# Moving thirteen of sixteen scalings by 1/rms from VectorE to GpSimd in two norm passages

## The chip, the cores and the metric

The kernel runs on one core of one Trainium2 chip. The metric is the device time of one execution in microseconds (us). The kernel before took 3422.58 us, the median of three runs between 3416.58 and 3427.88 us. PE is TensorE, PEld its weight loads, DVE is VectorE, ACT is ScalarE, POOL is GpSimd, SP is SyncE, which here issues the DMAs.

## The reference

A block of three layers on one sequence of 512 tokens with 2048 channels: an S5 layer, a FoX attention layer, and a layer that mixes dilated attention with RWKV-7. Two of the places between them matter here. Each of the first two layers ends with a projection whose output is normed and added to the residual stream, and what comes next norms the sum again:

```
def rmsnorm(x, g):
    xf = x.astype(F32)
    y = xf * lax.rsqrt(jnp.mean(xf * xf, axis=-1, keepdims=True) + RMS_EPS)
    return (y * g.astype(F32)).astype(x.dtype)
...
return h + rmsnorm(y @ w_out, g_post)     # end of the S5 layer
kvf = rmsnorm(h, g_kv) @ w_kv             # what reads it next
...
return h + rmsnorm(o @ w_out, g_post)     # end of the FoX layer
h = rms_norm(x, norm_g[l])                # what reads it next
proj = jnp.matmul(h, w_in[l])
```

## The kernel before

All activations lie transposed: 2048 channels are 16 blocks of 128 partitions, and each block is 128x512 (512 tokens), f32. `g1` holds the residual stream h in 16 blocks, `g2` the projection's output in 16 blocks. A projection works on 228 weight tiles of 128x2048, one after the other. To get the accuracy of f32 from TensorE's fp32r matmuls, the weight tile and the activations are each split in a high part (rounded, by ACT: `whi`, `rhi`) and a low part (the rest: `wlo`, by GpSimd in `make_lo`; `rlo`, by DVE), and each 128x128 piece of a tile takes three matmuls (`project`, L158 to L160). A tile's two buffers alternate.

The two norm passages lie around tile 64 (`N_GATE`, the forget gate's weights, passage 1) and tile 145 (`N_LORA`, passage 2). Each goes like this:

- PE sums the squares over the partitions (L660), ACT takes the root (L664), DVE the reciprocal (L669). In the passages the reciprocal is written to a PSUM bank, `banks[6]`, and not back to `rstd` in SBUF.
- DVE runs `residual_and_split`: for block k it adds the scaled output to the residual (L769), scales the next block (`scaled(k+1)`, L763, `g2` times `banks[6]`), and, once ACT has rounded the new residual to `rhi` (L791 or L793), subtracts to get `rlo` (L774 in passage 1, L776 with the gain in passage 2).
- ACT runs `split_after_update`: when a block of the residual is up, it makes `rhi` and the block's square (L795).
- PE runs `project_summing`: for each block, once `rlo` is there, three matmuls of the tile, and one with ones that sums the squares of the next norm (L784). PE does nothing else in the passage.

Semaphores order the engines; each engine runs its own list, written out by hand. `h_sc` counts scaled blocks, `h_up` added ones, `r_hi` and `r_lo` the split parts. On GpSimd's list, passage 1 has `make_lo` of tile 65 and then `scale_w` of tile 66, which multiplies the weights with a gain (L839, four instructions). Passage 2 has `make_lo` of tile 146; `make_lo` of tile 147 waits for ACT, which makes that tile's `whi` after the passage.

What follows the passages: after passage 1, ACT's root, DVE's reciprocal and the gate's chain come ahead of ACT's `whi` of tile 66 (L139), GpSimd's `wlo` of it, and then PE's tile. After passage 2, SP waits for `r_lo`, stores h to HBM (L1874) and loads tables, for which DVE's first step of the third layer waits.

Of the kernel before, what the change touches and what calls it, by code (L numbers as in the profile page):

```python
# [17 lines left out]
ALU = mybir.AluOpType  # L18
# [6 lines left out]
KT = D // P  # L25
# [48 lines left out]
def program(nc, a):  # L74
    ctx = ExitStack()
    with ctx:
# [3 lines left out]
        def sem(name):  # L80
            return ctx.enter_context(nc.semaphore(name))
# [8 lines left out]
        g2 = sb("g2", [P, KT * T])  # L90
# [3 lines left out]
        rstd = sb("rstd", [P, T])  # L94
# [4 lines left out]
        banks = [bank[:, i, :] for i in range(8)]  # L99
# [41 lines left out]
        def make_lo(pool, n, slot):  # L141
            pool.wait_ge(w_hi, n + 1)
            for q in range(QUARTERS):
                c = slice(q * D // QUARTERS, (q + 1) * D // QUARTERS)
                ins = pool.tensor_tensor(wlo[:, slot, c], wraw[:, slot, c], whi[:, slot, c].bitcast(F32), ALU.subtract)  # L145
            ins.then_inc(w_lo, 1)
# [97 lines left out]
        def col(base, k):  # L244

            if isinstance(k, int):
                return base[:, k * T:(k + 1) * T]
            return base[:, bass.ts(k, T)]
# [418 lines left out]
        def norm_recip(d, link, which, out=None):  # L667
            d.wait_ge(st_sd, which + 1)
            d.reciprocal(rstd[:, :] if out is None else out, rstd[:, :]).then_inc(st_rd, 1)  # L669
            d.wait_ge(st_rd, which + 1)  # L670
# [5 lines left out]
        h_sc = sem("h_sc")  # L676
# [76 lines left out]
        def dve_out_squares(d, n0, sbase):  # L753
            dve_square(d, 0, n0 % 2, sbase, first=True)
            dve_square(d, 1, (n0 + 1) % 2, sbase)
            with d.Fori(0, 7) as i:
                for u in range(2):
                    dve_square(d, 2 * i + (2 + u), (n0 + u) % 2, sbase)

        def residual_and_split(d, n, hbase, rgain, rbase):  # L760

            def scaled(k):
                d.tensor_tensor(col(g2, k), col(g2, k), banks[6], ALU.mult).then_inc(h_sc, 1)  # L763
            d.wait_ge(evac, n + 2)
            scaled(0)
            for k in range(KT):
                c = col(g1, k)
                d.wait_ge(h_sc, hbase + k + 1)
                d.tensor_tensor(c, c, col(g2, k), ALU.add).then_inc(h_up, 1)  # L769
                if k < KT - 1:  # L770
                    scaled(k + 1)
                d.wait_ge(r_hi, rbase + k + 1)
                if rgain is None:
                    d.tensor_tensor(rlo[:, k, :], c, rhi[:, k, :].bitcast(F32), ALU.subtract).then_inc(r_lo, 1)  # L774
                else:
                    d.scalar_tensor_tensor(rlo[:, k, :], c, vec[:, rgain + k:rgain + k + 1],  # L776
                                           rhi[:, k, :].bitcast(F32), ALU.mult, ALU.subtract).then_inc(r_lo, 1)
# [54 lines left out]
        def scale_w(pool, n, slot, half, gain):  # L832

            pool.wait_ge(w_in[slot], 16 * half + 16)
            raw = wraw[:, slot, :].rearrange("p (k c) -> p k c", k=KT)
            for q in range(QUARTERS):
                k = slice(q * KT // QUARTERS, (q + 1) * KT // QUARTERS)
                g = vec[:, gain + q * KT // QUARTERS:gain + (q + 1) * KT // QUARTERS]
                ins = pool.tensor_tensor(raw[:, k, :], raw[:, k, :], bc(g, 2, [P, KT // QUARTERS, P]), ALU.mult)  # L839
            ins.then_inc(w_sc, 1)  # L840
# [1051 lines left out]
        @block.gpsimd  # L1892
        def _(pool):
            pool.memset(ones[:, :], 1.0).then_inc(t_zero, 1)
            pool.wait_ge(cst, 48)
            for n in range(EARLY + 1):
                make_lo(pool, n, n % 2)
            pool.wait_ge(pw_rdy, 1)
            for v in range(2):
                pool.memset(m8b[v].rearrange("q (g k) -> q g k", g=GT)[:, :, 0:1], 0.0)  # L1900
            pool.memset(m["tt"], 0.0).then_inc(t_zero, 1)
            pool.wait_ge(t_zero, 2)
            steps(pool, pool_step)
            tile_pairs(pool, 32, 62, pool_lo)
            for n in (62, 63):
                make_lo(pool, n + 1, 1 - n % 2)
                scale_w(pool, n + 2, n % 2, (n + 2) // 2, V_GKV)
            make_lo(pool, 65, 1)
            scale_w(pool, 66, 0, 33, V_GKV)
            with pool.Fori(0, KT - 1) as h:  # L1910
                fox_pool(pool, h)
            fox_pool(pool, KT - 1, last=True)
            tile_pairs(pool, 130, 146, lambda p, n, u, h, j: make_lo(p, n, u))
            make_lo(pool, 146, 0)
            make_lo(pool, 147, 1)
            tile_pairs(pool, 148, 152, lambda p, n, u, h, j: make_lo(p, n, u))
            make_lo(pool, 152, 0)
            with pool.Fori(0, 7) as p:
                rw_pool(pool, p, True)
            rw_pool(pool, 7, False)  # L1920
            make_lo(pool, 213, 1)
            at_pool(pool)
            tile_pairs(pool, 214, 228, lambda p, n, u, h, j: make_lo(p, n, u))
# [85 lines left out]
        @block.vector  # L2009
        def _(d):  # L2010
            link = Chain(d, vch)
            d.sem_inc(evac, 2)
            d.sem_inc(a_wr, 16)
            d.wait_ge(cst, 48)
            parameters(d, link, 0)
            split_lo(d, g1, V_G1, 0, (sqb0, 0))
            norm_recip(d, link, 0)
            parameters(d, link, 1)
            d.wait_ge(e_wr, 16)
            d.wait_ge(t_zero, 2)  # L2020
            steps(d, dve_step, link, DVE_U_LINKS)
            d.wait_ge(z_rdy, 15)
            d.wait_ge(gemm, N_GLU)
            d.tensor_tensor(zt, acc[1][:, :], rstd[:, :], ALU.mult).then_inc(evac, 1)
            split_lo(d, g1, None, 16)
            d.wait_ge(z_in, 32)
            d.wait_ge(z_rdy, KT)
            tile_pairs(d, 32, 48, lambda d, n, u, h, j: dve_glu(d, link, n, u, h, j), link, 2)
            split_lo(d, g2, None, 32)
            dve_out_squares(d, N_WO, 16)  # L2030
            norm_recip(d, link, 1, banks[6])
            d.wait_ge(x_in, 64)
            residual_and_split(d, N_GATE, 0, None, 48)
            norm_recip(d, link, 2)
            gate_dve(d, link)
            d.wait_ge(msk_in, 16)
            fox_dve(d, link, 0, False)
            fox_dve(d, link, 1, True)
            with d.Fori(2, KT) as h:
                link.enter(h - 2, 4)  # L2040
                fox_dve(d, link, h, True)
                link.leave(KT - 2)
            softmax_max(d, link, KT - 1)
            split_lo(d, g2, None, 64, ks=range(0, 6))
            softmax_divide(d, link, KT - 1)
            split_lo(d, g2, None, 64, ks=range(6, 10))
            gate_out(d, KT - 1)
            split_lo(d, g2, None, 64, ks=range(10, KT))
            dve_out_squares(d, N_FO, 48)
            norm_recip(d, link, 3, banks[6])  # L2050
            residual_and_split(d, N_LORA, 16, V_G2, 80)
            norm_recip(d, link, 4)

            link(d.memset(w["u"][:, 0:1], 0.0))
            d.wait_ge(x_out, 64)
            d.wait_ge(p6_in, 96)
            for i, name in enumerate(("wa", "sg0", "sg1")):
                shift_mix(d, link, N_LORA + i, (N_LORA + i) % 2, vec[:, V_MU + i:V_MU + i + 1], w[name], lo_u, (lo_u, i))
            d.wait_ge(lo_u, 3)
            for i in range(3):  # L2060
                rw_inputs(d, link, 0, i)
            rw_z(d, 0)
            d.memset(xt["zt3"], 0.0)
            for name in ("rcos", "rsin"):
                ins = d.tensor_tensor(xt[name], xt[name], rstd[:, :], ALU.mult)
            link(ins)
            with d.Fori(0, 7) as p:
                link.enter(p, RW_LINKS)
                rw_dve(d, link, p, True)
                link.leave(7)  # L2070
            rw_dve(d, link, 7, False)
            at_dve(d, link)
            d.wait_ge(x_in, 80)
            dve_last(d, link, 212, 0, 0, 80, first=True)
            dve_last(d, link, 213, 1, 1, 80)
            d.wait_ge(f_x, 48)
            tile_pairs(d, 214, 228, lambda d, n, u, h, j: dve_last(d, link, n, u, j + 2, 80))
            norm_recip(d, link, 5)
            for k in range(KT):
                c = g1[:, k * T:(k + 1) * T]  # L2080
                d.scalar_tensor_tensor(c, c, vec[:, V_GF + k:V_GF + k + 1], rstd[:, :], ALU.mult, ALU.mult)\
                 .then_inc(f_r, 1)
# [191 lines left out]
```

## Time and profile before

| | |
|---|---|
| median of three runs | 3422.58 us |
| the profiled execution | 3420.76 us |
| its span in the trace | 3418.9 us |
| PE busy | 3244.8 us (95%) |
| DVE busy | 1400.2 us (41%) |
| ACT busy | 1119.1 us (33%) |
| POOL busy | 1657.1 us (48%) |

The busy share of an engine is over the whole span. The two passages are short stretches of it: from PE's sum of squares to its last L784 they lie at 936 to 979 us and at 1991 to 2035 us. A row of the timeline tells when an instruction started, how long it took from its start to its end, and in brackets how long its engine sat idle before it and what ended that. The duration of an instruction holds the time in which it had started and waited for its operands' port.

### The profile page before, as it was taken

How to read it: one execution, taken by the hardware profiler on the slowest of the kernel's cores; microseconds unless marked ns; L12 is line 12 of the kernel's file. 1: busy time of each engine (PE TensorE's matmuls, PEld its weight loads, DVE VectorE, ACT ScalarE, POOL GpSimd, SP SyncE). 2: the span in 40 equal slices, each digit the busy share in tenths (PEclk: the TensorE clock that was granted, in tenths of full speed). 3: DMA queues.
4: the chain of work that ended last, by engine and by line, in shares of the span. 5: the costliest groups of instructions: out<-in, count | busy, mean ns of one | idle time of the engine just before them, and what ended most of it. 6: DMA issues, size and time to landing. Idle time of an engine off the chain costs nothing.

```text
span 3418.9 us, 48576 instructions
## 1 busy us (share of the span) xinstructions
PE 3244.8 (95%) x18636; PEld 2523.1 (74%) x18636; DVE 1400.2 (41%) x2138; ACT 1119.1 (33%) x1472; POOL 1657.1 (48%) x1315
## 2 busy tenths in 40 slices
PE   5899998999989999999998978999999999999997
PEld 3688886878757877877887856777777777774686
DVE  8877784120052222222312043444445445355512
ACT  4344443233333233223323233233233233234421
POOL 2466652444547776776663414443344344442242
PEclk9899998999999999999999999999999999997999
DMA  3555556232212222222221222222222222223322
GB/s 132 153 147 163 165 159 171 98 136 98 98 50 87 82 78 86 86 84 76 86 86 63 97 108 99 82 77 83 81 96 75 83 84 83 75 84 107 115 94 91
DMA packets 122898, 341.60 MB, mean 100 GB/s; under 512 B 59408, under 2 KB 62480, under 8 KB 91664
## 3 DMA queue, kind: packets, MB, share of 16 engines
q1 hardware_dynamic: 122768, 339.67, 30.1%
q8 instruction: 106, 1.74, 0.2%
q14 instruction: 24, 0.20, 0.0%
HBM read 301.09 MB, written 33.82 MB: 98 GB/s over the span
## 4 chain that ended last, share of the span: by engine, by line
PE 80%; issue 10%; POOL 5%; DVE 4%; ACT 2%; DMA 0%; ACTq 0%; SPq 0%; POOLq 0%; DVEq 0%
PE bank L158 22%; PE bank L160 21%; PE bank L159 20%; POOL wlo L145 4%; PE bank L1321 3%; PE bank L1629 2%; PE bank L1008 1%; PE bank L1026 1%; PE bank L421 1%; PE bank L420 1%; ACT whi L139 1%; PE bank L1630 1%; PE bank L406 1%; PE bank L432 1%; PE bank L1704 1%
## 5 line engine op out<-in xcount | busy, mean ns | idle before, releaser
L145 POOL TENSOR_TENSOR wlo<-wraw,whi 128x512 fp32r<-128x512 f32 x912 | 1245.4, 1397 | 1473.6 <-ACT whi L139 1473.5
L158 PE MATMUL bank<-rhi,whi 128*128 128x512 f32 x3648 | 1494.3, 410 | 109.2 <-POOL wlo L145 38.6
L159 PE MATMUL bank<-rlo,whi 128*128 128x512 f32 x3648 | 1433.4, 393 | 0.0
L160 PE MATMUL bank<-rhi,wlo 128*128 128x512 f32 x3648 | 1432.7, 393 | 0.0
L158 PEld LDWEIGHTS bank<-rhi,whi 128*128 128x128 f32 x3648 | 691.7, 190 | 326.7 <-issue 91.1
L160 PEld LDWEIGHTS bank<-rhi,wlo 128*128 128x128 f32 x3648 | 691.7, 190 | 149.6
L159 PEld LDWEIGHTS bank<-rlo,whi 128*128 128x128 f32 x3648 | 693.1, 190 | 140.9 <-issue 11.3
L139 ACT ACTIVATE whi<-wraw 128x2048 fp32r<-128x2048 f32 x228 | 436.9, 1916 | 624.4 <-PE bank L160 479.9
L839 POOL TENSOR_TENSOR wraw<-wraw,vec 128x512 f32<-128x512 f32 x260 | 266.1, 1055 | 0.0
L751 DVE TENSOR_TENSOR ssum<-ssum,wk 128x512 f32<-128x512 f32 x30 | 21.6, 719 | 311.8 <-ACT wk L741 311.8
L741 ACT ACTIVATE wk<-bank 128x512 f32<-128x512 f32 x32 | 27.9, 871 | 238.0 <-PE bank L160 238.0
L1321 PEld LDWEIGHTS bank<-g 64*64 64x64 f32 x2560 | 82.0, 134 | 30.2 <-issue 29.4
L1530 POOL TENSOR_TENSOR g<-g,wk 128x256 f32<-128x256 f32 x80 | 58.4, 752 | 91.9 <-PE bank L1321 66.1
L1215 DVE TENSOR_TENSOR g<-g,bank 128x256 f32<-128x256 f32 x80 | 32.4, 405 | 161.9 <-PE bank L1321 161.6
L1321 PE MATMUL bank<-g 64*64 64x64 f32 x2560 | 93.6, 221 | 0.2
L913 DVE SCALAR_TENSOR_TENSOR wk<-bank,rstd 128x512 f32<-128x512 f32 x16 | 11.1, 692 | 200.1 <-PE bank L160 200.1
L918 DVE TENSOR_TENSOR wk<-bank,rstd 128x512 f32<-128x512 f32 x16 | 11.1, 692 | 168.7 <-PE bank L160 168.7
L728 DVE TENSOR_TENSOR wk<-wk,g 128x512 f32<-128x512 f32 x16 | 11.1, 693 | 149.2 <-ACT wk L724 142.0
L1480 ACT ACTIVATE g<-bank 128x256 f32<-128x256 f32 x80 | 30.7, 384 | 124.2 <-PE bank L1321 121.5
L929 ACT ACTIVATE wk<-wk 128x128 f32<-128x128 f32 (+1 forms) x64 | 35.2, 551 | 108.5 <-DVE wk L887 108.5
L1100 DVE TENSOR_TENSOR wk<-bank,rstd 128x512 f32<-128x512 f32 x27 | 18.6, 691 | 117.5 <-PE bank L160 104.3
L1809 DVE TENSOR_TENSOR g<-g,bank 128x512 f32 (+1 forms) x16 | 11.0, 688 | 135.4 <-PE bank L160 135.4
(361 smaller groups left out, 3277.9 us busy)
## 6 DMA issues: line engine op xcount, KB each, us to landing
wraw<-in_wall_dram SPq DMA_DIRECT2D x228, 1024.0 KB, 4.8
g<-in_bmat_dram SPq DMA_DIRECT2D x16, 512.0 KB, 5.5
g<-scr_e SPq DMA_DIRECT2D x128, 64.0 KB, 4.8
scr_a<-ssum SPq DMA_DIRECT2D x24, 256.0 KB, 2.1
g<-in_xp_dram SPq DMA_DIRECT2D x4, 1024.0 KB, 12.5
g<-in_cmat_dram SPq DMA_DIRECT2D x16, 256.0 KB, 4.5
scr_u<-wk SPq DMA_DIRECT2D x16, 256.0 KB, 5.8
scr_y<-wk SPq DMA_DIRECT2D x16, 256.0 KB, 2.2
```

The lines of the kernel that those rows point to most:

```text
L139: act.activation(whi[:, slot, :], wraw[:, slot, :], ACT.Copy).then_inc(w_hi, 1)
L145: ins = pool.tensor_tensor(wlo[:, slot, c], wraw[:, slot, c], whi[:, slot, c].bitcast(F32), ALU.subtract)
L158: pe.matmul(acc[slot][:, :], whk, rhi[:, k, :], start=(k == 0), stop=False)
L159: pe.matmul(acc[slot][:, :], whk, rlo[:, k, :], start=False, stop=False)
L160: ins = pe.matmul(acc[slot][:, :], wlk, rhi[:, k, :], start=False, stop=(k == KT - 1))
L406: ins = pe.matmul(ps_k[g // 4][0:SC, (g % 4) * P:(g % 4 + 1) * P], m["bb"][:, g * SC:(g + 1) * SC], q1[v][:, g * 144:g * 144 + P], start=T ...
L420: pe.matmul(ps_y[:, cols], m["tt"][:, g * P:(g + 1) * P], ug[u][:, cols], start=True, stop=False)
L839: ins = pool.tensor_tensor(raw[:, k, :], raw[:, k, :], bc(g, 2, [P, KT // QUARTERS, P]), ALU.mult)
L929: ins = act.activation(sc, sc, ACT.Exp, bias=mf["nm"][:, b:b + 1], accum_out=mf["sum"][:, b:b + 1])
L1321: ins = pe.matmul(to[hs_[e], b * CH:(b + 1) * CH], lhs[hs_[e], b * CH:(b + 1) * CH], rhs[hs_[e], b * CH:(b + 1) * CH], start=True, stop=True)
L1530: pool.tensor_tensor(ml[hd].rearrange("p (b t) -> p b t", b=NB), ab4[hd][:, :, 0], bc(lv, 1, [P, NB, CH]), ALU.mult).then_inc(rw_ml, 1)
L1629: pe.matmul(to, at_q[u][hs_[hd], b * P:(b + 1) * P], at_k[u][hs_[hd], 0:n], start=True, stop=False)
```

## The change

From the fourth block on (k of 3 to 15), GpSimd does the scaling in both passages. DVE keeps the scaling of blocks 0 to 2, all additions and all low parts. GpSimd's new piece stands in its list behind `make_lo` of tile 65 and ahead of `scale_w` of tile 66 in passage 1, and behind `make_lo` of tile 146 in passage 2. It starts when DVE's three scalings have counted `h_sc` up. The reciprocal goes back to `rstd` in SBUF, and all scalings, those on DVE too, read it there.

```
+        OWN = 3
+
+        def scaled(eng, k):
+            eng.tensor_tensor(col(g2, k), col(g2, k), rstd[:, :], ALU.mult).then_inc(h_sc, 1)
+
+        def scale_out(pool, hbase):
+            pool.wait_ge(h_sc, hbase + OWN)
+            for k in range(OWN, KT):
+                scaled(pool, k)
+
         def residual_and_split(d, n, hbase, rgain, rbase):
 
-            def scaled(k):
-                d.tensor_tensor(col(g2, k), col(g2, k), banks[6], ALU.mult).then_inc(h_sc, 1)
             d.wait_ge(evac, n + 2)
-            scaled(0)
+            scaled(d, 0)
             for k in range(KT):
                 c = col(g1, k)
                 d.wait_ge(h_sc, hbase + k + 1)
                 d.tensor_tensor(c, c, col(g2, k), ALU.add).then_inc(h_up, 1)
-                if k < KT - 1:
-                    scaled(k + 1)
+                if k + 1 < OWN:
+                    scaled(d, k + 1)
                 d.wait_ge(r_hi, rbase + k + 1)
...
             make_lo(pool, 65, 1)
+            scale_out(pool, 0)
             scale_w(pool, 66, 0, 33, V_GKV)
...
             make_lo(pool, 146, 0)
+            scale_out(pool, 16)
             make_lo(pool, 147, 1)
...
-            norm_recip(d, link, 1, banks[6])
+            norm_recip(d, link, 1)
...
-            norm_recip(d, link, 3, banks[6])
+            norm_recip(d, link, 3)
```

DVE's list before, from the reciprocal of passage 1 (L763 scales, L769 adds, L774 makes the low part):

```order
L669 RECIPROCAL bank<-rstd 128x512 [waits st_sd]
L763 TENSOR_TENSOR g<-g,bank 128x512 [waits evac,x_in,st_rd]
L769 TENSOR_TENSOR g<-g 128x512 [waits h_sc]
L763 TENSOR_TENSOR g<-g,bank 128x512
L774 TENSOR_TENSOR rlo<-g,rhi 128x512 [waits r_hi]
L769 TENSOR_TENSOR g<-g 128x512 [waits h_sc]
```

The same place in the changed kernel, where the addition is L777 and the low part L782:

```order
L669 RECIPROCAL rstd<-rstd 128x512 [waits st_sd]
L763 TENSOR_TENSOR g<-g,rstd 128x512 [waits evac,x_in,st_rd]
L777 TENSOR_TENSOR g<-g 128x512 [waits h_sc]
L763 TENSOR_TENSOR g<-g,rstd 128x512
L782 TENSOR_TENSOR rlo<-g,rhi 128x512 [waits r_hi]
L777 TENSOR_TENSOR g<-g 128x512 [waits h_sc]
L763 TENSOR_TENSOR g<-g,rstd 128x512
L782 TENSOR_TENSOR rlo<-g,rhi 128x512 [waits r_hi]
L777 TENSOR_TENSOR g<-g 128x512 [waits h_sc]
L782 TENSOR_TENSOR rlo<-g,rhi 128x512 [waits r_hi]
L777 TENSOR_TENSOR g<-g 128x512 [waits h_sc]
L782 TENSOR_TENSOR rlo<-g,rhi 128x512 [waits r_hi]
```

After the third scaling DVE's list is additions and low parts in turn, each with its wait.

GpSimd's list before, at passage 1 (L145 is `make_lo`, L839 is `scale_w`):

```order
L145 TENSOR_TENSOR wlo<-wraw,whi 128x512 [waits w_hi]
L145 TENSOR_TENSOR wlo<-wraw,whi 128x512 x3
L839 TENSOR_TENSOR wraw<-wraw,vec 128x512 [waits w_in0]
L839 TENSOR_TENSOR wraw<-wraw,vec 128x512 x3
L1910 UNCONDITIONAL_BRANCH
```

The same place in the changed kernel, where `scale_w` is L847:

```order
L145 TENSOR_TENSOR wlo<-wraw,whi 128x512 [waits w_hi]
L145 TENSOR_TENSOR wlo<-wraw,whi 128x512 x3
L763 TENSOR_TENSOR g<-g,rstd 128x512 [waits h_sc]
L763 TENSOR_TENSOR g<-g,rstd 128x512 x12
L847 TENSOR_TENSOR wraw<-wraw,vec 128x512 [waits w_in0]
L847 TENSOR_TENSOR wraw<-wraw,vec 128x512 x3
L1919 UNCONDITIONAL_BRANCH
```

Thirteen instructions come in between, each with both inputs in SBUF, and one wait, for DVE's third scaling.

## Rows read from the trace of the kernel before

**Rows 1.** Timeline of all engines, one block of passage 1, GpSimd idle: start us, duration us, engine
```profile
955.36 0.68 DVE L769 TENSOR_TENSOR g<-g 128x512 f32<-128x512 f32 x1
955.50 0.50 PE L158 MATMUL bank<-rhi,whi 128*128 128x512 f32 x1 [0.17 <-DVE rlo L774]
...
955.96 0.68 DVE L763 TENSOR_TENSOR g<-g,bank 128x512 f32<-128x512 f32 x1
956.08 0.63 ACT L791 ACTIVATE rhi<-g 128x512 fp32r<-128x512 f32 x1 [0.84 <-DVE g L769]
...
956.31 1.02 PE L784 MATMUL bank<-wk,ones 128*128 128x512 f32 x2
...
956.74 0.69 DVE L774 TENSOR_TENSOR rlo<-g,rhi 128x512 fp32r<-128x512 f32 x1
957.35 0.69 DVE L769 TENSOR_TENSOR g<-g 128x512 f32<-128x512 f32 x1
```

**Rows 2.** Timeline of DVE, blocks of passage 2, GpSimd idle
```profile
2013.61 0.69 DVE L769 TENSOR_TENSOR g<-g 128x512 f32<-128x512 f32 x1
...
2015.08 0.75 DVE L776 SCALAR_TENSOR_TENSOR rlo<-g,vec,rhi 128x512 fp32r<-128x512 f32 x1 [0.19 <-ACT rhi L793]
2015.75 0.68 DVE L769 TENSOR_TENSOR g<-g 128x512 f32<-128x512 f32 x1
```

**Rows 3.** Timeline of GpSimd, passage 1, and two of its instructions apart
```profile
939.88 5.84 POOL L145 TENSOR_TENSOR wlo<-wraw,whi 128x512 fp32r<-128x512 f32 x4 [3.09 <-ACT whi L139]
945.68 5.83 POOL L839 TENSOR_TENSOR wraw<-wraw,vec 128x512 f32<-128x512 f32 x4
...
942.33 3.39 POOL L145 TENSOR_TENSOR wlo<-wraw,whi 128x512 fp32r<-128x512 f32 x2
```

**Rows 4.** Timeline of DVE, passage 1, while GpSimd works
```profile
941.43 0.69 DVE L763 TENSOR_TENSOR g<-g,bank 128x512 f32<-128x512 f32 x1
...
947.64 1.52 DVE L769 TENSOR_TENSOR g<-g 128x512 f32<-128x512 f32 x1
949.09 0.67 DVE L763 TENSOR_TENSOR g<-g,bank 128x512 f32<-128x512 f32 x1
...
950.54 1.52 DVE L769 TENSOR_TENSOR g<-g 128x512 f32<-128x512 f32 x1
```

**Rows 5.** Instructions by line on GpSimd, duration ns: least, median, most
```profile
L485 POOL TENSOR_TENSOR wk<-wk,g x16: 1301/1524/2335, 107.1 to 508.2; 128x512 f32<-128x512 f32 x16
L839 POOL TENSOR_TENSOR wraw<-wraw,vec x260: 1033/1041/1488, 921.2 to 1768.2; 128x512 f32<-128x512 f32 x130
L145 POOL TENSOR_TENSOR wlo<-wraw,whi x912: 1255/1288/3682, 16.0 to 3383.3; 128x512 fp32r<-128x512 f32 x183
```

**Rows 6.** Timeline of DVE, passage 1: the low part of block 9
```profile
964.70 0.69 DVE L774 TENSOR_TENSOR rlo<-g,rhi 128x512 fp32r<-128x512 f32 x1
```

**Rows 7.** Timeline of GpSimd and DVE, start of passage 2
```profile
1995.04 5.84 POOL L145 TENSOR_TENSOR wlo<-wraw,whi 128x512 fp32r<-128x512 f32 x4 [7.91 <-ACT whi L139]
1996.59 0.69 DVE L763 TENSOR_TENSOR g<-g,bank 128x512 f32<-128x512 f32 x1
```

**Rows 8.** Timeline behind passage 1: what waits for its end
```profile
979.25 0.69 ACT L664 ACTIVATE rstd<-bank,vec 128x512 f32<-128x512 f32 x1 [2.11 <-PE bank L784]
...
994.82 0.79 PE L158 MATMUL bank<-rhi,whi 128*128 128x512 f32 x1 [4.70 <-POOL wlo L145]
```

**Rows 9.** Timeline behind passage 2
```profile
2034.95 3.42 SPq L1874 DMA_DIRECT2D scr_x<-g  x4
...
2062.08 0.80 PE L158 MATMUL bank<-rhi,whi 128*128 128x512 f32 x1 [16.31 <-POOL wlo L145]
```

**Rows 10.** Stretches of passage 1: us, PE, PEld, DVE, ACT, POOL busy, granted clock, DMA
```profile
950.00:953.00 3.00, 1.93 (x6) 0.86 (x5) 2.90 (x4) 1.26 (x3) 1.51 (x2) 1.00 0.01 3
```

**Rows 11.** Timeline of PE, first block of passage 1, at the low clock
```profile
944.74 0.77 PE L158 MATMUL bank<-rhi,whi 128*128 128x512 f32 x1 [7.66 <-DVE rlo L774]
946.16 1.91 PE L784 MATMUL bank<-wk,ones 128*128 128x512 f32 x2
```

## The prediction

> **What bounds the kernel now.** I read the page first: PE is busy for 95% of the span, so a change to DVE's and GpSimd's work counts only where PE waits for them. In the two norm passages it does. There the timeline is read block by block. In a block of passage 1 with GpSimd idle [rows 1] PE starts at 955.50 after 0.17 us of waiting for DVE's `rlo`, and its last matmul ends at 956.31 + 1.02 = 957.33, so a block costs PE 1.83 us. The blocks follow each other at 957.35 - 955.36 = 1.99 us. What sets 1.99 is a loop through ACT: DVE starts the addition at 955.36, ACT starts `rhi` at 956.08, DVE starts `rlo` at 956.74 (1.38 after the addition), and the next addition at 957.35. DVE's scaling lies at 955.96 to 956.64, inside the wait for ACT's `rhi`, which ends at 956.08 + 0.63 = 956.71. It ends 0.1 us before `rlo` can start and so costs nothing. In passage 2 the same holds with more room [rows 2]: the period is 2015.75 - 2013.61 = 2.14 us, and `rlo` still waits 0.19 us for ACT behind the scaling.
>
> A second thing is to be seen where GpSimd works beside DVE [rows 3, 4]. The addition, which needs 0.68 us alone, takes 1.52 us, and two of them follow at 950.54 - 947.64 = 2.90 us. GpSimd's four instructions of L839 take 5.83 us there, 1.45 each, where one takes 1.04 alone [rows 5]. In one block DVE does two instructions with both inputs in SBUF (addition and `rlo`) and GpSimd two of its own, and 2 x 1.45 = 2.90: they take turns, one waiting for the other. The scaling, which reads PSUM, stays at 0.67 us in the same stretch [rows 4]. The Trainium skill states this as a rule (SBUF — State Buffer, "Who interferes with whom"): a DVE instruction with two SBUF inputs and a GpSimd instruction that reads SBUF share one read port, which the first one holds for its whole instruction. By that rule, the trace agrees, and it speaks against this change, which gives DVE's scalings a second SBUF input and puts thirteen more port holders beside DVE.
>
> **What the change removes.** Thirteen DVE scalings per passage, at 0.60 us of DVE's time each. I cost their removal at 0, because the loop through ACT stays as it is and covers them [rows 1, 2]: without them DVE waits 0.78 us for ACT instead of 0.17. The reciprocal keeps its size and its place; I cost its new target at 0.
>
> **What it adds on GpSimd.** Thirteen multiplications 128x512 with two full inputs. Nearest rows: L839, whose second input is a repeated vector, 1.04 us alone; L145, two full inputs, 1.26 us; L485, two full inputs and an f32 output, 1.30 us [rows 5]. Taking turns with DVE, two instructions of L145 need 945.72 - 942.33 = 3.39 us less the overlap of 0.04 [rows 3], that is 1.67 each; L839 needs 1.45; L485 by 1.30 plus the same 0.42 of DVE's hold would need 1.72 or 1.75. I take 1.67, since two full inputs are what the new ones have, and keep 1.45 and 1.75 as the ends. [...]
>
> GpSimd takes two blocks in the time in which DVE takes one, so it is never late with a block. What it does is to lengthen DVE's loop from 1.99 or 2.14 to 3.34 us for as long as it works.
>
> **Passage 1.** The start: GpSimd's `make_lo` of tile 65 runs from 939.88 [rows 3], with boundaries at 942.33, 944.0 (halfway) and 945.7 once each instruction has DVE's turn in it. DVE's scaling of block 0, ready at 941.43 [rows 4], now gets the port at 942.33, the addition at 944.0, the scaling of block 1 at 945.7. Then at DVE's own spacing of 0.61: `rlo` of block 0 at 946.33, addition 1 at 946.94, the scaling of block 2 at 947.55, done at 948.23. GpSimd starts there, and `rlo` of block 1, ready 1.38 after its addition at 948.32, comes just behind it. From 948.25 on there are 13 instructions at 1.67 and the 4 of `scale_w` at 1.45, together 27.5 us; two go to a block, so `rlo` of block 9 gets its port after the seventeenth, at 948.25 + 27.5 - 0.42 = 975.3. Before, it started at 964.70 [rows 6], `scale_w`'s contention included. From block 10 on the pace is 1.99 again. Passage 1: **+10.6**.
>
> **Passage 2.** GpSimd's `make_lo` starts at 1995.04 and DVE's first scaling at 1996.59 [rows 7]; the same reckoning (port at 1997.48, 1999.2, 2000.88) ends the third scaling at 2003.45. Before, GpSimd was then idle. Thirteen at 1.67 less 0.42 end at 2024.7, where `rlo` of block 7 gets its port; before it started at 2015.08 [rows 2]. Passage 2: **+9.7**.
>
> **Does it reach the end?** PE waits for `rlo` in nearly every block, so its last L784 moves with the last `rlo`. Behind passage 1 ACT's root waits for that matmul, and the gate's chain leads from there to the `wlo` for which PE waits 4.70 us until 994.82 [rows 8]. Behind passage 2 the stores start at 2034.95, when the last low part and sums are there, and PE waits 16.31 us for what follows from them [rows 9]. No slack takes the delay up. GpSimd's delayed work costs nothing: `scale_w` of tile 66 ends near 976, and ACT wants it after the gate's chain; `make_lo` of tile 147 waits for ACT until after passage 2. No DMA issue moves: `wlo` of tile 65 still comes ahead of the new piece, and it alone frees the buffer.
>
> **The sum.** +10.6 + 9.7 = +20.3, on the profiled 3420.76 gives 3441.1. The median of the runs is 1.8 above the profiled execution, so it is 3442.9, rounded 3443. With 1.45 in place of 1.67 it is 26 x 0.22 = 5.7 less (+14.6), with 1.75 it is 2.1 more (+22.4). With the runs' own scatter of 5 to 6 us this case reaches from 3433 to 3450.
>
> **Rivals.** (a) *The clock falls too.* In the long contended stretch PE works 1.83 of 3.34 us. In the one like it before it worked 1.93 of 3.00 us at a granted clock of 1.00 [rows 10], and the changed one is thinner. At half clock a block takes PE 946.16 + 1.91 - 944.74 = 3.33 us [rows 11], which hides behind 3.34; but if the clock is still low for the first two free blocks, each costs 1.34 more (1.19 in passage 2). That is +5.1 over both passages, less what PE regains at 0.16 and 0.31 per later block, so about +4: 3447. For it: the clock is at 0.50 when the passages begin, and PE is idle more. Against it: the clock stayed high in that stretch. The Trainium skill (TensorE: Matmul & The Clock Gate, "What's actually happening") says that a low rate comes from too little recent activity; no run here yet shows this stretch.
>
> (b) *The port isn't what slows DVE*, and the 1.52 us are of those weight tiles alone. Then only the start costs, addition 1 at 946.94 in place of the time when it got its port, 945.7, thus 1.2 per passage: 3425, no change that can be measured. Against it: the addition takes 1.52 us beside GpSimd and 0.68 without it [rows 1, 4], the scaling from PSUM doesn't grow, and GpSimd's own grow from 1.04 to 1.45.
>
> (c) *Faster: DVE is the bound of the passage, not ACT's loop.* If `rlo` could follow earlier with the scaling gone, the pace would fall to PE's own 1.83: 13 x (1.99 - 1.83) + 13 x (2.14 - 1.83) = 6.1 less, 3416.5. It decides once GpSimd's instructions take turns without holding DVE up, and `rlo` no longer waits for `rhi`. Against it are the 0.19 us of waiting for ACT in each block of passage 2 [rows 2], even with the scaling there.
>
> That the change doesn't do what it says can be left out: the lists show it.
>
> **Chances.** The forecast 0.75, (a) 0.13, (b) 0.08, (c) 0.04. A measurement of this kernel tells 0.3% (10.3 us) from no change. Slower by more than that: nearly all of the forecast (its low end, +14.6, less scatter can fall under 10.3, some 0.03) and all of (a): 0.85. Within 0.3%: (b) and that edge, 0.11. Faster: 0.04, and that only counts (c) with scatter on its side. The range reaches past the forecast's own on both sides for (a) and scatter: 3431 to 3453; (b) and (c) are left out with 0.12.
>
> **What would show it.** Right: additions of 1.5 to 1.8 us for blocks 2 to about 8 or 9, GpSimd's L763 at about 1.7 each, 13 in a row right behind DVE's third scaling, a pace of 3.3 us, then 1.99 and 2.14 unchanged to the end; the last L784 of passage 1 some 10 us later. Wrong: L763 on GpSimd at 1.5 or less (a smaller sum), additions at 0.68 us beside it (b), a pace under 1.99 us anywhere (c), a granted clock of 0.50 within the passage (a). A delay that is there in the passages and not behind them would mean that I missed slack.

## The result and the profile after

The changed kernel takes 3442.71 us, the median of seven runs (3440.9 to 3449.59), against 3422.58 us for the kernel before on the same chip (seven runs, 3416.58 to 3429.13). The ratio is 1.0059, with a 95% interval of 1.0047 to 1.0071: slower by 20 us, or 0.6%. The profiled execution took 21.5 us longer by its span (3440.4 against 3418.9 us).

DVE's timeline of passage 1 after the change (L763 scales, L777 adds, L782 makes the low part):

```profile
941.99 1.49 DVE L763 TENSOR_TENSOR g<-g,rstd 128x512 f32<-128x512 f32 x1
943.51 1.63 DVE L777 TENSOR_TENSOR g<-g 128x512 f32<-128x512 f32 x1
945.07 1.75 DVE L763 TENSOR_TENSOR g<-g,rstd 128x512 f32<-128x512 f32 x1
946.74 0.68 DVE L782 TENSOR_TENSOR rlo<-g,rhi 128x512 fp32r<-128x512 f32 x1
947.35 0.68 DVE L777 TENSOR_TENSOR g<-g 128x512 f32<-128x512 f32 x1
947.95 0.68 DVE L763 TENSOR_TENSOR g<-g,rstd 128x512 f32<-128x512 f32 x1
948.72 1.80 DVE L782 TENSOR_TENSOR rlo<-g,rhi 128x512 fp32r<-128x512 f32 x1
...
953.81 1.77 DVE L777 TENSOR_TENSOR g<-g 128x512 f32<-128x512 f32 x1
956.28 0.98 DVE L782 TENSOR_TENSOR rlo<-g,rhi 128x512 fp32r<-128x512 f32 x1 [0.70 <-ACT rhi L799]
957.18 1.77 DVE L777 TENSOR_TENSOR g<-g 128x512 f32<-128x512 f32 x1
...
975.76 0.75 DVE L782 TENSOR_TENSOR rlo<-g,rhi 128x512 fp32r<-128x512 f32 x1 [0.70 <-ACT rhi L799]
976.43 0.68 DVE L777 TENSOR_TENSOR g<-g 128x512 f32<-128x512 f32 x1
977.81 0.69 DVE L782 TENSOR_TENSOR rlo<-g,rhi 128x512 fp32r<-128x512 f32 x1 [0.70 <-ACT rhi L799]
978.42 0.68 DVE L777 TENSOR_TENSOR g<-g 128x512 f32<-128x512 f32 x1
```

GpSimd's timeline of the same passage:

```profile
940.45 5.83 POOL L145 TENSOR_TENSOR wlo<-wraw,whi 128x512 fp32r<-128x512 f32 x4 [3.09 <-ACT whi L139]
948.71 21.47 POOL L763 TENSOR_TENSOR g<-g,rstd 128x512 f32<-128x512 f32 x13 [2.44 <-DVE g L763]
970.14 5.82 POOL L847 TENSOR_TENSOR wraw<-wraw,vec 128x512 f32<-128x512 f32 x4
```

While GpSimd scales, the additions take 1.77 us and follow at 957.18 - 953.81 = 3.37 us; once GpSimd is done with `scale_w`, at 975.96, they take 0.68 us and follow at 978.42 - 976.43 = 1.99 us, as before [rows 1]. In that last part DVE waits 0.70 us for ACT in every block: the time of the scalings that it no longer does has turned into waiting. No row of DVE waits for a block that GpSimd has scaled. GpSimd's thirteen take 21.47 us, 1.65 each on average. The first two scalings on DVE, which read PSUM and took 0.69 us before [rows 4], now take 1.49 and 1.75 us beside `make_lo`.

To measure a passage I take the time from the start of the reciprocal ahead of it to the start of the reciprocal behind it. Of passage 1 and of passage 2 after the change:

```profile
938.60 3.35 DVE L669 RECIPROCAL rstd<-rstd 128x512 f32<-128x512 f32 x1 [2.14 <-ACT rstd L664]
...
991.11 3.35 DVE L669 RECIPROCAL rstd<-rstd 128x512 f32<-128x512 f32 x1 [2.65 <-ACT rstd L664]
2004.00 3.35 DVE L669 RECIPROCAL rstd<-rstd 128x512 f32<-128x512 f32 x1 [1.94 <-ACT rstd L664]
...
2055.97 3.35 DVE L669 RECIPROCAL rstd<-rstd 128x512 f32<-128x512 f32 x1 [2.63 <-ACT rstd L664]
```

and of the kernel before:

```profile
938.04 3.36 DVE L669 RECIPROCAL bank<-rstd 128x512 f32<-128x512 f32 x1 [2.14 <-ACT rstd L664]
...
979.97 3.35 DVE L669 RECIPROCAL rstd<-rstd 128x512 f32<-128x512 f32 x1 [2.62 <-ACT rstd L664]
1993.20 3.36 DVE L669 RECIPROCAL bank<-rstd 128x512 f32<-128x512 f32 x1 [1.94 <-ACT rstd L664]
...
2035.62 3.35 DVE L669 RECIPROCAL rstd<-rstd 128x512 f32<-128x512 f32 x1 [2.63 <-ACT rstd L664]
```

From start to start, passage 1 grew from 41.93 to 52.51 us (+10.6) and passage 2 from 42.42 to 51.97 us (+9.6), together 20.1 us. All that lies outside, the span less these two, went from 3334.6 to 3335.9 us. What comes behind a passage kept its length. These are PE's first matmuls after the wait behind passage 1 and behind passage 2, in the changed kernel:

```profile
1005.96 0.79 PE L158 MATMUL bank<-rhi,whi 128*128 128x512 f32 x1 [4.69 <-POOL wlo L145]
2082.26 0.80 PE L158 MATMUL bank<-rhi,whi 128*128 128x512 f32 x1 [16.12 <-POOL wlo L145]
```

From the second reciprocal to them it is 14.85 and 26.29 us, against 14.85 and 26.46 before [rows 8, 9].

### The profile page after: what moved, and what is told of

Its sections match the earlier page's. It is cut to its first block, busy times and chain, and to the rows that moved or that the text cites. A ratio compares the mean times of both kernels' runs of the same rounds, so it can differ in the third digit from the quotient of the medians.

```text
span 3440.4 us, 48576 instructions
## 1 busy us (share of the span) xinstructions
PE 3245.5 (94%) x18636; PEld 2523.4 (73%) x18636; DVE 1403.4 (41%) x2112; ACT 1119.3 (33%) x1472; POOL 1700.0 (49%) x1341
## 4 chain that ended last, share of the span: by engine, by line
PE 80%; issue 9%; POOL 5%; DVE 5%; ACT 2%; DMA 0%; ACTq 0%; SPq 0%; POOLq 0%; DVEq 0%
PE bank L158 22%; PE bank L159 21%; PE bank L160 21%; POOL wlo L145 3%; PE bank L1329 3%; PE bank L1637 2%; POOL g L763 1%; PE bank L1016 1%; PE bank L1034 1%; PE bank L421 1%; PE bank L420 1%; PE bank L1638 1%; PE bank L406 1%; PE bank L432 1%; ACT whi L139 1%
## 5 line engine op out<-in xcount | busy, mean ns | idle before, releaser
L145 POOL TENSOR_TENSOR wlo<-wraw,whi 128x512 fp32r<-128x512 f32 x912 | 1245.2, 1396 | 1446.1 <-ACT whi L139 1446.1
L847 POOL TENSOR_TENSOR wraw<-wraw,vec 128x512 f32<-128x512 f32 x260 | 266.1, 1055 | 0.0
```

## The experiments

The table gives for each kernel the two stretches just described, what they differ by from before (84.35 us together), and the span outside of them; these are from one profiled execution of each kernel. The times are medians of 4 (e5) to 12 (e7) runs. Each ratio is to the runs of before on the same chip, whose median was 3421.85 us beside e1 to e4, 3422.00 beside e5 to e7 and 3418.69 beside e8.

| kernel | passage 1, us | passage 2, us | together | outside | time, us | ratio, 95% interval |
|---|---|---|---|---|---|---|
| before | 41.93 | 42.42 | | 3334.6 | 3422.58 | |
| changed | 52.51 | 51.97 | +20.1 | 3335.9 | 3442.71 | 1.0059 [1.0047, 1.0071] |
| e1_nobody_scales | 41.92 | 42.42 | 0.0 | 3336.3 | 3424.38 | 1.0001 [0.9989, 1.0013] |
| e2_extra_multiplications | 48.23 | 48.20 | +12.1 | 3336.4 | 3436.09 | 1.0038 [1.0023, 1.0053] |
| e3_writes_only | 42.58 | 42.43 | +0.7 | 3334.3 | 3422.63 | 1.0007 [0.9997, 1.0018] |
| e4_all_on_dve_from_sbuf | 44.52 | 43.67 | +3.8 | 3342.0 | 3431.14 | 1.0022 [1.0011, 1.0034] |
| e5_two_buffers | 51.29 | 50.70 | +17.6 | 3342.2 | 3443.47 | 1.0052 [1.0034, 1.0070] |
| e6_own_nine | 48.37 | 48.29 | +12.3 | 3335.1 | 3436.28 | 1.0043 [1.0027, 1.0060] |
| e7_addition_ahead | 38.12 | 39.22 | -7.0 | 3333.6 | 3412.54 | 0.9981 [0.9968, 0.9993] |
| e8_one_per_block | 50.42 | 48.98 | +15.1 | 3332.2 | 3435.59 | 1.0051 [1.0035, 1.0067] |

The medians move by several us for a reason outside of the passages (last section), so the readings rest on the two stretches, and the times only bear them out.

**e1: is the removal worth anything?** The kernel before, without the scalings of blocks 3 to 15, which are added unscaled:

```
-                d.wait_ge(h_sc, hbase + k + 1)
+                if k < 3:
+                    d.wait_ge(h_sc, hbase + k + 1)
...
-                if k < KT - 1:
+                if k + 1 < 3:
                     scaled(k + 1)
```

> The kernel before, but blocks 3 to 15 of the projection's output are added unscaled in both passages: DVE does only the scalings of blocks 0 to 2, from PSUM, and GpSimd gets nothing new. The scaling of 13 blocks is left out. Theory (DVE's scaling is hidden behind ACT's rounding of the same block): paces stay 1.99 us in passage 1 and 2.14 us in passage 2, the last low part starts where it did, the time is that of before within 2 us (3422). Rival (DVE is the bound of the passage, so that taking scalings off it gains): the pace falls towards 1.83 us, 6 us less, 3416.

Both stretches are the same to 0.01 us. DVE's timeline in passage 1:

```profile
958.20 0.68 DVE L770 TENSOR_TENSOR g<-g 128x512 f32<-128x512 f32 x1
959.58 0.69 DVE L775 TENSOR_TENSOR rlo<-g,rhi 128x512 fp32r<-128x512 f32 x1 [0.70 <-ACT rhi L792]
960.19 0.68 DVE L770 TENSOR_TENSOR g<-g 128x512 f32<-128x512 f32 x1
```

With nothing between the addition and the low part the period is still 960.19 - 958.20 = 1.99 us, and where the scaling lay DVE now idles 0.70 us until ACT's `rhi` is there. So the removal alone, with nothing new on GpSimd, is worth nothing.

**e2: does GpSimd's work cost if nobody needs it?** The kernel before, with 13 multiplications more on GpSimd in each passage, on a scratch tensor:

```
+        NX = 13
...
+        def extra(pool, hbase, base):
+            pool.wait_ge(h_sc, hbase + 3)
+            for i in range(NX):
+                pool.wait_ge(ex, base + i)
+                pool.tensor_tensor(scr[:, :], scr[:, :], scr[:, :], ALU.mult).then_inc(ex, 1)
```

> The kernel before, with all scalings on DVE from PSUM, plus 13 GpSimd multiplications 128x512 per passage on a scratch tensor of their own, in the place of the new scalings, started by DVE's third scaling. DVE never waits for their data. Theory (they take turns with DVE at a shared SBUF port): the contended blocks follow at 3.3 us, additions take 1.5 to 1.8 us, +9 us in passage 1 and +8 us in passage 2 against before, since DVE's own scalings read PSUM and the start stays as it was; 3439 to 3440. Rival (DVE is late in the changed kernel because it waits for blocks that GpSimd has scaled, by semaphore): here there is no such wait, 3422 to 3425.

The stretches grew by 6.3 and 5.8 us, without DVE waiting for any result of GpSimd: the mechanism is as expected, its size is not. The reason is in the instruction itself (GpSimd, durations in ns, least, median and most):

```profile
L786 POOL TENSOR_TENSOR scr<-scr x26: 1039/1368/1465, 946.4 to 2026.8; 128x512 f32<-128x512 f32 x26
```

A multiplication whose two inputs are the same buffer takes 1.04 us at the least, like L839 with its repeated vector, and not the 1.26 us of L145 [rows 5]. That left open whether those of the changed kernel take longer because they read two buffers.

**e5: the same with two buffers.** One change against e2 (and a wait on ACT behind the passage, for the buffer's sake):

```
-                pool.tensor_tensor(scr[:, :], scr[:, :], scr[:, :], ALU.mult).then_inc(ex, 1)
+                pool.tensor_tensor(scr[:, :], scr[:, :], whi[:, slot, 0:512].bitcast(F32), ALU.mult).then_inc(ex, 1)
```

> e2 again, with one thing changed: the 13 extra GpSimd multiplications read two different buffers (scratch and a piece of whi), where those of e2 read the same buffer twice. In e2 each took 1.41 us beside DVE, in the changed kernel 1.65. Theory (GpSimd's price hangs on how many operands it fetches through the port): 1.65 us each, +8.8 us in passage 1 and +7.8 us in passage 2 over before, 3438 to 3440. Rival (the 1.65 us of the changed kernel come from something in its g2 blocks or semaphores): 1.41 us again, +12 us in all, 3434.

GpSimd's timeline, passage 1:

```profile
947.72 21.47 POOL L786 TENSOR_TENSOR scr<-scr,whi 128x512 f32<-128x512 f32 x13 [1.22 <-DVE g L766]
```

The thirteen take 21.47 us, to the hundredth what the changed kernel's own take. The stretches grew by 9.4 and 8.3 us, 17.6 together, where 16.6 were expected. The time of 3443.47 us lies above the 3438 to 3440 expected; the last section looks at that. So 17.6 of the 20.1 us are there when DVE's arithmetic is just as before and all it has to bear is a neighbour that reads two buffers.

**e3: is it reading, or any work of GpSimd's?** As e2, but with 34 memsets, which read nothing:

```
+        NX = 34
...
+            for i in range(NX):
+                pool.wait_ge(ex, base + i)
+                pool.memset(scr[:, :], 1.0).then_inc(ex, 1)
```

> The kernel before plus 34 GpSimd memsets 128x512 per passage, which write SBUF and read nothing, in the same place and for about as long (16 to 20 us of GpSimd). Theory (what is contended for is the read port of DVE's second SBUF input): the memsets leave DVE alone, additions stay at 0.68 us behind make_lo, and the time is that of before within 2 us, 3422 to 3425. Rival (any GpSimd instruction on SBUF holds DVE up, or GpSimd's semaphores do): additions of 1 us and more, +8 to +17 us, 3431 to 3440.

GpSimd is busy for 19.78 us of passage 1, and DVE does not notice:

```profile
946.49 19.78 POOL L786 MEMSET scr<- 128x512 f32 x34 [1.21 <-DVE g L766]
```

```profile
957.10 0.68 DVE L772 TENSOR_TENSOR g<-g 128x512 f32<-128x512 f32 x1
957.70 0.68 DVE L766 TENSOR_TENSOR g<-g,bank 128x512 f32<-128x512 f32 x1
958.48 0.69 DVE L777 TENSOR_TENSOR rlo<-g,rhi 128x512 fp32r<-128x512 f32 x1
959.09 0.68 DVE L772 TENSOR_TENSOR g<-g 128x512 f32<-128x512 f32 x1
```

The period is 1.99 us, passage 2 grew by 0.01 us and passage 1 by 0.65. The growth of passage 1 is no work of the memsets: `scale_w` comes later there, behind them, at 966.24, and its first instruction holds up a low part that would have taken 0.69 us:

```profile
966.45 1.38 DVE L777 TENSOR_TENSOR rlo<-g,rhi 128x512 fp32r<-128x512 f32 x1
```

The memsets wrote SBUF all that time, and GpSimd waited for a semaphore before each. So what costs is GpSimd's reading.

**e4: what does reading rstd in SBUF cost?** The changed kernel with `OWN = KT` and without the two calls of `scale_out`:

```
-        OWN = 3
+        OWN = KT
```

> The changed kernel with all 16 scalings on DVE, nothing new on GpSimd: what is left of the change is that the scalings read rstd in SBUF and not the PSUM bank. Theory: only the stretches in which GpSimd does make_lo and scale_w beside DVE cost more, because DVE's scalings now take turns too: about +3 us in passage 1 (it still has scale_w) and +1.5 us in passage 2, 3426 to 3428. The paces with GpSimd idle stay 1.99 and 2.14 us. Rival (most of the 20 us comes from reading rstd in SBUF): 3435 or more.

The stretches grew by 2.6 and 1.3 us, near the expected 3 and 1.5, and with GpSimd idle the pace is the old one. The time of 3431.14 us is above the 3426 to 3428 expected; in the profiled execution 7.4 us of its growth lie outside the passages, which the last section looks at. In the changed kernel only three scalings per passage are left on DVE, so it pays only the part of the start. The trace has that part: from the start of the first scaling to that of the third it takes 947.95 - 941.99 = 5.96 us in passage 1, and before 4.77:

```profile
946.20 0.68 DVE L763 TENSOR_TENSOR g<-g,bank 128x512 f32<-128x512 f32 x1
```

In passage 2 it takes 6.01 us against 4.76. That is 2.4 us for both passages, and with the 17.6 of e5 for the neighbour it makes 20.0 of the 20.1 us.

**e6: does the cost follow the number?** The changed kernel with `OWN = 9`, so that seven scalings go to GpSimd.

> The changed kernel with OWN = 9: DVE scales blocks 0 to 8, GpSimd only the last seven, started by DVE's ninth scaling. Theory (each GpSimd multiplication beside DVE costs half of 3.34 less the free pace, 0.67 us in passage 1 and 0.60 in passage 2, on top of the start that e4 showed): +6.7 us and +6.1 us, 3435. Rival (the cost is a fixed one of handing over between the engines, whatever the number of blocks): +10 us each, 3442.

The stretches grew by 6.4 and 5.9 us, 12.3 together, against 12.8 expected. From 13 to 7 instructions per passage 7.8 us went away, 0.65 for each, which agrees with half of the difference between 3.37 us and the free pace of 1.99 or 2.14 us (0.62 to 0.69).

**e8: the same work, spread.** GpSimd waits before each scaling for the addition of the block two before:

```
             for k in range(OWN, KT):
+                pool.wait_ge(h_up, hbase + k - 1)
                 scaled(pool, k)
```

> The changed kernel, but GpSimd waits before each of its 13 scalings until DVE has added the block two before it (h_up). The same instructions on each engine, 13 more waits per passage, and one GpSimd instruction to a block where there were two. Theory (the cost is the port, and part of a GpSimd instruction can lie in the 0.7 to 0.8 us in which DVE waits for ACT): each multiplication, 1.22 us, starts when the addition has left the port and holds rlo up by 1.27 less 0.70, so the pace is 2.5 to 2.6 us for all blocks from 1 on in place of 3.34 for seven or eight of them; +7 to +8 us in each passage, +15 us in all, 3437, 5 us less than the changed kernel. Rival (handing blocks over by semaphore costs): with more waits and with every block fetched just in time it gets slower than the changed kernel, over 3445.

The stretches grew by 8.5 and 6.6 us, 15.1 against 20.1 in the changed kernel. The timelines of DVE and GpSimd:

```profile
956.52 0.68 DVE L778 TENSOR_TENSOR g<-g 128x512 f32<-128x512 f32 x1
957.27 1.28 POOL L763 TENSOR_TENSOR g<-g,rstd 128x512 f32<-128x512 f32 x1 [1.23 <-DVE g L778]
957.89 1.22 DVE L783 TENSOR_TENSOR rlo<-g,rhi 128x512 fp32r<-128x512 f32 x1 [0.70 <-ACT rhi L800]
959.03 0.68 DVE L778 TENSOR_TENSOR g<-g 128x512 f32<-128x512 f32 x1
```

The period is 959.03 - 956.52 = 2.51 us. GpSimd's instruction now takes 1.28 us and starts right behind the addition. Some 0.6 us of it, from 957.27 to 957.89, lie in DVE's wait for ACT, and the rest holds the low part up, which takes 1.22 us in place of 0.69. There are more waits by semaphore and less time, so handing over is not what costs. It is still slower than before, since that rest lengthens every block. By the interval of its ratio the time can't be told from that of the changed kernel; by the stretches it can.

**e7: a version that takes out the loop instead.** All scalings on DVE from PSUM, the addition of block k+1 and the scaling of k+2 ahead of the low part of k; and `scale_w` of tile 66 behind the passage:

```
+            for k in range(1, KT):
+                if k < KT - 1:
+                    add(k + 1)
+                if k < KT - 2:
+                    scaled(k + 2)
+                low(k)
...
             make_lo(pool, 65, 1)
+            pool.wait_ge(r_lo, 64)
             scale_w(pool, 66, 0, 33, V_GKV)
```

> The kernel before, all scalings on DVE from PSUM, with DVE's order skewed: the addition of block k+1 and the scaling of k+2 stand ahead of the low part of block k, so that DVE works through ACT's rounding; and GpSimd's scale_w of tile 66 waits until passage 1 is over. Theory (ACT's loop sets 1.99 and 2.14 us, and PE's own 1.83 us a block comes right behind it): the loop is gone, PE never waits once it has started, and the passages end 1 to 2 us earlier each, 3419 to 3420, no change that can be measured. Rival (PE could go faster than 1.83 us a block when it is fed): more than 5 us.

It is faster than both kernels, by a little: 0.9981 [0.9968, 0.9993] of before, with the stretches 3.8 and 3.2 us shorter. DVE's three instructions now follow without a gap:

```profile
957.78 0.69 DVE L769 TENSOR_TENSOR g<-g 128x512 f32<-128x512 f32 x1
958.38 0.68 DVE L763 TENSOR_TENSOR g<-g,bank 128x512 f32<-128x512 f32 x1
958.98 0.69 DVE L775 TENSOR_TENSOR rlo<-g,rhi 128x512 fp32r<-128x512 f32 x1
959.58 0.68 DVE L769 TENSOR_TENSOR g<-g 128x512 f32<-128x512 f32 x1
```

The period is 1.80 us, three instructions at 0.60, so DVE itself is now what sets the pace here. The expectation of 1 to 2 us per passage was too small, and the rival was right in this: PE can go faster than 1.83 us a block. Its timeline, where it has blocks waiting:

```profile
956.70 0.80 PE L158 MATMUL bank<-rhi,whi 128*128 128x512 f32 x1
957.80 1.02 PE L797 MATMUL bank<-wk,ones 128*128 128x512 f32 x2
958.26 0.79 PE L158 MATMUL bank<-rhi,whi 128*128 128x512 f32 x1
```

Fed, a block takes PE 958.26 - 956.70 = 1.56 us. The rows of the trace overlap when matmuls follow each other, and a block's time from its first start to its last end is longer than what it takes of PE. In passage 2 only DVE's order was changed, so its 3.2 us come from the order alone; how passage 1's 3.8 us divide between the order and the later `scale_w` wasn't tried.

## Why the prediction was right

The forecast was 3443, measured 3442.7, and its steps hold one by one. The hit that counts is the +20.1 us of the two stretches against the forecast +20.3. That the median agrees to 0.3 us is luck, since runs of the same kernel lie 12 us apart.

- **Removal at 0.** Shown by e1 to 0.01 us per passage. The wait for ACT that takes the scaling's place was put at 0.78 us and is 0.70. The 0.17 us given for the wait with the scaling there is PE's for `rlo`; DVE's low part starts only 0.1 us behind the scaling's end [rows 1].
- **The port.** The adding and the low part take turns with GpSimd's reading instructions, and the pace was to go to 3.34 us; it is 3.37. That it is reading, not work on GpSimd as such, is shown by e3; that no handing over is needed for it, by e2 and e5. The rule cited from the Trainium skill (SBUF — State Buffer, "Who interferes with whom") says that an instruction which only writes does not contend; by that rule, the trace of e3 agrees. On how long the port is held, the prediction's sentence goes further than the rows: two GpSimd and two DVE instructions go into 3.37 us, and a GpSimd instruction takes 1.26 us alone, which leaves 3.37 / 2 - 1.26, about 0.4 us, for a DVE instruction whose row is 0.68 us long. This is an estimate; what DVE holds of the port is in no row.
- **The price of a multiplication.** 1.67 us was taken, between 1.45 and 1.75; it is 21.47 / 13 = 1.65. In the steady part it is 3.37 / 2 = 1.68; the first of the thirteen has no DVE instruction ahead of it. e2 and e5 show why L145 and not L839 was the row to go by: two different buffers.
- **The start.** GpSimd's start was put at 948.25; less the drift of 0.56 us with which this passage began (941.99 against 941.43), it is 948.15. The last contended low part was put at 975.3, and starts at 975.76, or 975.2 without the drift.
- **Passage 1 +10.6, passage 2 +9.7.** Measured +10.6 and +9.6 (9.55).
- **No slack behind.** Slack would have shortened what follows a passage. From the second reciprocal to PE's next tile it stayed at 14.85 us behind passage 1 and lost 0.17 us behind passage 2.

**The rivals.** (a), a falling clock: PE does idle more, and the granted clock was low a little longer at the start, but inside the long contended stretch it stayed at 1.00:

```profile
950.00:952.80 2.80, 2.80 (x6) 1.49 (x5) 2.21 (x2) 0.56 (x2) 2.80 (x2) 0.50 0.18 76
953.00:970.00 17.00, 9.57 (x27) 4.30 (x25) 13.52 (x11) 5.90 (x11) 17.00 (x11) 1.00 0.00 0
```

(Stretches of passage 1 after the change; the columns are those of [rows 10].) PE worked for 9.57 of 17 us at the high one of its two levels, 2.4 GHz. The low clock before it cost nothing: after two blocks at that clock PE still waited for DVE at the third:

```profile
953.94 0.49 PE L158 MATMUL bank<-rhi,whi 128*128 128x512 f32 x1 [0.51 <-DVE rlo L782]
```

Nor did it at the end: from the start of the last low part to the reciprocal behind it, it is 3.32 to 3.39 us in both passages of every kernel but e7, where it is 5.22 us because PE is still working off blocks that are ready.

(b), another cause for the long additions, is refuted by e2, e5 and e3. (c), DVE as the bound, is refuted by e1. The price given for it, and the sentence that a block costs PE 1.83 us, were wrong: e7 shows 1.56 us. The forecast didn't rest on that figure, since in it PE always waits for DVE.

## What to carry to other kernels

Before moving work to an idle engine, look for what the busy one does in the gap: here DVE's scalings lay in its wait for ACT and cost nothing, so there was nothing to win. What did cost was the neighbour. A DVE instruction with two SBUF inputs that meets a GpSimd instruction which reads SBUF waits for it, whatever data the two work on: the additions went from 0.68 to 1.77 us. Here a DVE instruction with one input in PSUM stayed out of this (0.67 us beside GpSimd [rows 4]), and GpSimd read for less where DVE waited for ACT anyway (e8). If an engine works through its list in order and waits for another engine in each step of a loop, try to put the next step's work ahead of the wait, as e7 does.

## What the runs showed of the hardware

- GpSimd's multiplication 128x512 f32 took 1.04 us at the least when both inputs were one buffer (e2) and 1.26 us when they were two (e5: 1263 ns at the least; e8: 1267 to 1282 ns for all 26). Memsets of that size took 0.53 us and didn't disturb DVE (e3).
- The executions differ by 5 to 10 us outside of the passages, in steps. In the third layer, behind 3070 us, the granted clock is low for a long stretch, and how long varies between the profiled executions. Stretches of the kernel before, and of e5 (columns as in [rows 10]):

```profile
3073.00:3119.00 46.00, 40.09 (x122) 21.02 (x121) 22.42 (x41) 16.75 (x43) 13.25 (x8) 0.50 0.38 120
3121.00:3131.00 10.00, 10.00 (x49) 5.04 (x47) 5.43 (x13) 3.68 (x12) 0.00 (x0) 1.00 0.15 31
```

```profile
3095.00:3141.00 46.00, 41.10 (x114) 20.73 (x111) 22.78 (x44) 17.36 (x44) 11.14 (x6) 0.50 0.38 120
3141.00:3150.00 9.00, 9.00 (x25) 5.43 (x24) 1.87 (x4) 2.63 (x10) 0.00 (x0) 0.50 0.00 0
3153.00:3163.00 10.00, 9.62 (x42) 5.01 (x38) 5.46 (x13) 4.04 (x13) 1.21 (x1) 1.00 0.56 158
```

  In e5 the clock stayed at 0.50 for some 10 us more, with PE fully busy in the last 9, and in e4 it did so too. e5 and e4 are the two whose span outside the passages is 3342 us, where the other eight lie between 3332 and 3336. In the profiled executions of e7 and e8 the low stretch was shorter, 34 and 38 us, in the other six about 48. Why it ends sooner or later wasn't tried, and that the edits have no part in it isn't shown; but the runs of the kernel before cluster as well, mostly near 3418, 3422 and 3428 us. It may be why the medians of e4 and e5 lie higher than their passages explain: the profiles show it for one execution of each.
